# Weight ring and residual placed 64 bytes higher in SBUF, the tiles behind them left where they are

## The reference, cut to what matters

```python
def swiglu(x, w_in, w_out):
    a, b = jnp.split(x @ w_in, 2, axis=-1)       # w_in 1024 x 5632
    return (jax.nn.silu(a) * b) @ w_out          # w_out 2816 x 1024
x = x + 0.5 * swiglu(rms_norm(x, ffn1_norm[l]), ffn1_w_in[l], ffn1_w_out[l])
```

## Time and profile before

| | us |
|---|---|
| median of 3 runs | 1806.16 (1805.4 to 1807.96) |
| the profiled execution's own time | 1801.17 |
| its span, first to last instruction | 1799.0 |
| PE busy | 1764.0 (98%) |
| PEld busy | 1631.4 (91%) |
| DVE busy | 1090.3 (61%) |
| ACT busy | 920.8 (51%) |
| POOL busy | 36.3 (2%) |
| granted TensorE clock, mean | 0.995 |

### The profile page before, as it was taken

The page is one execution under the profiler, slowest core; times in us unless marked ns, Lnnn a source line. Parts: engine busy times, 40 slices in busy tenths (PEclk is TensorE's granted clock), DMA queues, the critical chain, the costliest instruction groups (busy, mean ns, idle before and its releaser), DMA issues.

```text
span 1799.0 us, 31794 instructions
## 1 busy us (share of the span) xinstructions
PE 1764.0 (98%) x12924; PEld 1631.4 (91%) x12924; DVE 1090.3 (61%) x1457; ACT 920.8 (51%) x1218; POOL 36.3 (2%) x60
## 2 busy tenths in 40 slices
PE   8999999999999999999999999999999999999998
PEld 8999877999999998888899999999989888989997
DVE  6555776655565565666676555755574657676554
ACT  5344565544444345476755444544454566654433
POOL 0000220000000000000000000000000000000000
PEclk9999999999999999999999999999999999999999
DMA  7555523555565545443355555555545443446552
GB/s 307 197 189 193 179 98 137 211 188 199 193 214 202 191 164 195 172 164 138 139 187 179 189 193 202 185 209 188 202 176 177 179 164 98 161 155 216 202 187 94
DMA packets 46689, 324.34 MB, mean 180 GB/s; under 512 B 5392, under 2 KB 5648, under 8 KB 8464
## 3 DMA queue, kind: packets, MB, share of 16 engines
q1 hardware_dynamic: 44208, 315.81, 48.9%
q10 hardware_dynamic: 2400, 7.38, 1.1%
HBM read 322.12 MB, written 1.05 MB: 180 GB/s over the span
## 4 chain that ended last, share of the span: by engine, by line
PE 91%; ACT 4%; DVE 3%; issue 1%; DMA 0%; POOL 0%; ACTq 0%; DVEq 0%; POOLq 0%
PE work L1525 20%; PE work L1527 20%; PE work L1526 20%; PE acc L1527 7%; PE acc L1526 7%; PE acc L1525 7%; PE work L1579 4%; PE acc L1776 2%; DVE lo L1012 1%; PE acc L1758 1%; ACT hi L610 1%; ACT prob L731 1%; PE acc L1768 1%; PE work L1626 0%; PE acc L1635 0%
## 5 line engine op out<-in xcount | busy, mean ns | idle before, releaser
L1012 DVE TENSOR_TENSOR lo<-raw,hi 128x2048 fp32r<-128x2048 f32 x280 | 640.3, 2291 | 345.4 <-ACT hi L610 344.8
L1525 PE MATMUL work<-xT_hi,hi 128*128 128x256 f32 x2656 | 739.0, 278 | 6.9 <-DVE lo L1012 6.8
L1527 PE MATMUL work<-xT_hi,lo 128*128 128x256 f32 x2656 | 734.8, 277 | 0.0
L1526 PE MATMUL work<-xT_lo,hi 128*128 128x256 f32 x2656 | 734.8, 277 | 0.0
L610 ACT ACTIVATE hi<-raw 128x2048 fp32r<-128x2048 f32 x280 | 534.9, 1914 | 387.9 <-PE work L1527 360.8
L1525 PEld LDWEIGHTS work<-xT_hi,hi 128*128 128x128 f32 x2656 | 499.4, 188 | 16.5 <-ACT headT L721 6.1
L1526 PEld LDWEIGHTS work<-xT_lo,hi 128*128 128x128 f32 x2656 | 499.5, 188 | 2.5
L1527 PEld LDWEIGHTS work<-xT_hi,lo 128*128 128x128 f32 x2656 | 499.4, 188 | 0.0
L1527 PE MATMUL acc<-hi,hT_lo 128*128 128x512 f32 x480 | 189.1, 394 | 0.0
L1526 PE MATMUL acc<-lo,hT_hi 128*128 128x512 f32 x480 | 188.2, 392 | 0.0
L1525 PE MATMUL acc<-hi,hT_hi 128*128 128x512 f32 x480 | 186.8, 389 | 0.0
(11 more groups left out here) (278 smaller groups left out, 2036.0 us busy)
## 6 DMA issues: line engine op xcount, KB each, us to landing
raw<-stream SPq DMA_DIRECT2D x298, 1024.0 KB, 4.8
mem_in<-mem ACTq DMA_DIRECT2D x3, 1024.0 KB, 6.4
post<-post ACTq DMA_DIRECT2D x6, 512.0 KB, 3.8
x<-x SPq DMA_DIRECT2D x2, 512.0 KB, 4.4
out<-x SPq DMA_DIRECT2D x4, 256.0 KB, 2.1
alibi<-alibi ACTq DMA_DIRECT2D x1, 768.0 KB, 9.5
params<-l_params SPq DMA_DIRECT2D x2, 328.0 KB, 5.3
params<-b_params SPq DMA_DIRECT2D x1, 534.0 KB, 10.0
```

The lines of the kernel that those rows point to most:

```text
L1012: nc.vector.tensor_tensor(lo[:, s, :], raw[:, s, :], hi[:, s, :].bitcast(F32), ALU.subtract).then_inc(lo_ready, 1)
L1525: nc.tensor.matmul(dst, a_hi, b_hi, start=start, stop=False)
L1526: nc.tensor.matmul(dst, a_hi, b_lo, start=False, stop=False)
L1527: return nc.tensor.matmul(dst, a_lo, b_hi, start=False, stop=stop)
```

## The change

One line is added in front of the ring: 64 bytes are left free. `raw`, `hi`, `lo`, `x`, `xs`/`heads1`/`rot` and `params` move up by 64 bytes, to 64 modulo 128 (`raw` from byte 16512 to 16576). `params` takes 4368 bytes and ends at 111056 instead of 110992, below `X_AT` = 111424, so `xT_hi` and all behind it keep their addresses. No instruction, wait, transfer, size or order is changed.

```diff
@@ -237,6 +237,7 @@
         def new(name, shape, dtype=F32):
             return place(name, shape, room(4 * int(np.prod(shape[1:]))), dtype)
 
+        room(64)
         raw = new("raw", [P, RING, UNIT])
         hi = new("hi", [P, RING, UNIT], F32R)
         lo = new("lo", [P, RING, UNIT], F32R)
```

## The result

The changed kernel took 1849.16 us (median of 4 runs, 1847.63 to 1851.79) against 1805.78 us before: ratio 1.0244, 95% interval 1.0228 to 1.0261. The profiled execution has a span of 1846.3 us, 47.3 us more than before.

The account below looks back on a forecast made before the run. PE, busy 98% of the span, was taken as the bound through the distance of its matmuls' starts. All terms summed to 0 on the profiled 1801.17 us, which lay 5 us below the median: forecast 1806 us, range 1795 to 1830.

Parts of the forecast that it names:

- the collision's cap: Upper price of operand streams colliding in one half, at all 11,616 full products: 3.4 ns each, +39 us, 1845 us.
- Absolute address: Matmuls: the half of the 128 bytes in which the moving operand starts costs nothing at 256 columns; 0.
- The two operands against each other: Full products, one operand at 0 and one at 64 before, both at 64 after: taken as 0, bounds -41 to +39 us.
- two nearest rows: Gate product and transposes in the trace, both read as showing 0 for operands in the same half, each with one gap.
- Its cap: Upper bound on full products from the trace's slowest steady pace, 0.1167 against 0.1133: 3.4 ns each, +39 us.
- the rival of the straight stretches: Code outside loops: long straight stretches shift phase, a random few tenths of a us; counted inside "no change" (0.57).
- 512 columns: The 2,304 matmuls of 512 columns: taken as 0, could vanish or grow by 8 us.
- 3 ns more for the same columns: One 512-column matmul takes 0.230 us, two of 256 take 0.2267; if tied to the ring's place, -8 us or as much more.
- Splits and transfers: ACT and DVE splits -6 to +6 ns each, value 0; transfers at most 0.7 us on a 4.8 us landing, hidden, 0.
- the collision of the two streams: Rival: at all 11,616 full products, both streams in one half stall PE; 1.7 ns each, +20 us, 1826 us; chance 0.25.

Follow-up runs that it names:

- e1_both64: Against the kernel before: ring, residual and params 64 bytes up as in the change, and X_AT 64 bytes up too; 1803.52 us, ratio 0.9993.
- e3_res64: Against the kernel before: only x, xs/heads1/rot and params moved by 64 bytes, raw, hi and lo left in place; 1805.36 us, ratio 1.0006.
- m1_pairs: Separate kernel without the computation: rows of fp32r matmuls on PE alone, moving and stationary tiles at chosen offsets; 256 columns 120.0 ns at 0/0, 113.4 at 0/192.
- e4_ring128: Against the kernel before: ring, residual and params 128 bytes up, distance from xT to ring 192 modulo 256 instead of 64; 1840.98 us, ratio 1.0215.
- e10_hT64: Against the kernel before: only hT, hT_last and all behind them moved 64 bytes up, ring and xT left in place; 1820.16 us, ratio 1.0086.
- e2_x64: Against the kernel before: only xT and what is behind it moved 64 bytes up, ring left in place; 1851.32 us, ratio 1.0249.
- m2_order: Separate kernel without the computation: PE alone in the kernel's own matmul order, weight tiles at distances 0, 64, 128, 192; 120.0, 117.7, 120.0, 117.7 ns, distance 64 also 113.3.

## Why the prediction was wrong

The forecast was no change, 1806 us, and the range ended at 1830; the time was 1849, above even the 1845 of the collision's cap.

- *Absolute address, 0.* Right: e1_both64 has both sides elsewhere and the time of before, e3_res64 the residual's side.
- *The two operands against each other, 0.* This is the step that failed. It measures +43 us. I took 0 because two nearest rows showed none, and named the gap of each: the gate's loads were only 24 columns wide, and the transposes had slack on the moving side. Together these gaps were the whole question. The slack of the transposes was real: with 128 moving columns 24 matmuls take 2.79 us in m1_pairs at 0/0 and at 0/64 alike, while with 256 and 512 the two placements differ. Also, both rows vary the half of 128 bytes, and that isn't the quantity that counts (e4_ring128).
- *Its cap, 3.4 ns.* Too low: 5.4 ns in the loop. I took the pace of the branch products as the slowest that this form can have. But 117.8 ns is itself one of these patterns, the slow one of distance 64, and not the worst there is. In the prediction it "looks like a limit of issue; the addresses do not touch it"; the very products of rows 10 run at 113.3 ns in e10_hT64, 240 in a row without a loop and with their own addresses unchanged, and at 113.3 in e4_ring128. So it is no limit of issue, and the rival of the straight stretches was priced at nothing on a wrong reading.
- *512 columns, 0.* Wrong in size, inside its bounds: +3.3 ns, +8 us. The "3 ns more for the same columns" do hang on the distance: they vanish at 0 (e2_x64).
- *Splits and transfers, 0.* Right: 1911 and 2291 ns, 4.8 us.
- *The rival that came true* is the collision of the two streams, at 0.25. Its sign and place were right, all full products and no idle time. Its rule, "both in one half collide", was wrong: opposite halves at distance 192 lose 2.2% too. The Trainium skill (TensorE: Matmul & The Clock Gate, section Part 2: What happens when you issue a matmul) says that loading the next weights takes no read bandwidth from the running matmul, since PE has two independent read ports. The traces do not agree with what I made of it, a term of 0: with all other engines idle, moving only the load's address changed the pace from 113.4 to 120.0 ns at 256 columns and from 226.7 to 233.4 at 512 (m1_pairs).

The Trainium skill (TensorE: Matmul & The Clock Gate, section Wait — 56ns, not 53.3ns?) gives columns over 2.4 GHz plus about 2.5 ns from start to start; by it my estimate is 109.2 and 215.8 ns for 256 and 512 columns. No placement in these runs held that; the lowest were 113.3 and 226.7 ns, both 1.0625 times the columns over 2.4 GHz, at a granted clock of 1.00.

What is shown: the addresses of the two operands relative to each other, and the pattern at entry, set the pace, in PE alone; moving both together changes nothing (e1_both64). In the full kernels the distance modulo 256 tells which paces can occur; each distance other than 0 and 64 was seen in one kernel only, and in m1_pairs two placements with the same distance differ (0/192 and 64/0). What stays open is the structure behind it: why distances 64 and 192 have a clean pattern in this order of matmuls, why the FFN enters it at 64 and seldom at 192, and how one would steer the entry. The rest before the change, some 13% of the 256-column matmuls at 118 ns, would be worth about 5 us, an estimate from 0.13 x 9,312 x 4.5 ns.

## What to carry to other kernels

If PE is the bound and its matmuls follow each other without idle time, the relative address of the stationary and the moving operand is a parameter of the kernel: moving one buffer by 64 bytes was worth 2.4%, and it must be measured in the kernel's own sequence, since the clean pace of an isolated pair at distance 192 (m1_pairs) didn't carry over to the FFN. Put a new tile in front of others only together with what it is multiplied with, or in multiples of 256 bytes. And a row that says "no effect" bounds only the case it has: where just the unseen combination is what the change creates, its price belongs into the range at full size.

## What the runs showed that I had not expected

- Start-to-start times of fp32r matmuls with 256 columns settle into steady levels. The commonest are 113.3, 117.8 and 120.0 ns, each held over hundreds of matmuls; others are seen too, 118.7 in the changed kernel, 116.7 in m1_pairs at 32/0. At 512 columns they are 226.7, 229, 232 and 233 ns.
- At one and the same addresses both 113.3 and 117.8 ns hold, chosen by what ran before (m2_order at distance 64, the branch products of the kernel before and of e10_hT64).
- Making 1,584 matmuls faster by 2.4 ns made the kernel 0.9% slower, since those behind them changed pattern.
